# Last stage of a hybrid decoder step: who adds the expert outputs to the residual rows, VectorE or TensorE

## The reference, cut to what matters

```python
combine = (jax.nn.one_hot(g_idx, N_GROUPS)[:, :, None] * within[:, None, :] * g_w[:, :, None]).reshape(n, N_EXPERTS)
y = jnp.zeros((n, D_MODEL), jnp.float32)
for e in range(N_EXPERTS):
    hid = jax.nn.silu(t @ w_gate[e]) * (t @ w_up[e])
    y = y + combine[:, e:e + 1] * (hid @ w_down[e]).astype(jnp.float32)
...
xp = xp + hier_moe(rmsnorm(xp, norm_ffn_g[l]), *moe_args)
...
y_prompt = rmsnorm(xp, final_norm_g)
y_sample = rmsnorm(xs, final_norm_g)
```

## Time and profile before

| | |
|---|---|
| median of 3 runs | 716.06 us (715.21 to 717.71) |
| profiled execution | 715.4 us |
| its span, first to last instruction | 713.7 us |
| TensorE busy in the span | 692.3 us (97%) |
| VectorE, ScalarE, GpSimd busy | 555.3, 451.4, 152.3 us |
| mean granted TensorE clock | 0.997 |
| last matmul of the last expert, start of its group | 681.71 us |
| first load of `yy` issued | 687.89 us |
| last scaling ends, last store issued | 710.2 us |

### The profile page before, as it was taken

The page is one execution under the profiler, slowest core; times in us unless marked ns, Lnnn a source line. Parts: engine busy times, 40 slices in busy tenths (PEclk is TensorE's granted clock), DMA queues, the critical chain, the costliest instruction groups (busy, mean ns, idle before and its releaser), DMA issues.

```text
span 713.7 us, 11899 instructions
## 1 busy us (share of the span) xinstructions
PE 692.3 (97%) x3816; PEld 540.9 (76%) x3816; DVE 555.3 (78%) x890; ACT 451.4 (63%) x714; POOL 152.3 (21%) x157
## 2 busy tenths in 40 slices
PE   7999999999999999999988999999999999999995
PEld 4777777887778778777777888888888888888842
DVE  4775866866858875363887999999999999999857
ACT  7645354453465643122245888898889888898745
POOL 1010010110110131000014233333333333341114
PEclk9999999999999999999999999999999999999998
DMA  9993830330311626635339999999999999998758
GB/s 350 267 308 96 196 89 0 88 88 0 88 59 68 237 96 235 261 128 187 112 137 353 415 415 412 411 392 388 403 392 381 380 393 393 366 404 339 268 197 357
DMA packets 80922, 181.10 MB, mean 254 GB/s; under 512 B 41720, under 2 KB 45984, under 8 KB 72696
## 3 DMA queue, kind: packets, MB, share of 16 engines
q1 hardware_dynamic: 71384, 163.12, 63.0%
q0 software_dynamic: 9216, 16.93, 6.3%
q10 hardware_dynamic: 288, 0.62, 0.3%
HBM read 162.89 MB, written 34.39 MB: 276 GB/s over the span
## 4 chain that ended last, share of the span: by engine, by line
PE 85%; DVE 4%; DMA 4%; ACT 2%; issue 2%; SPq 1%; POOL 1%; DVEq 0%; ACTq 0%; POOLq 0%
PE psZ L1391 24%; PE psZ L901 20%; PE psS L1418 12%; PE psZ L1092 10%; PE psT L831 6%; PE psOG L831 2%; PE psOG L974 2%; PE psS L942 2%; DMA wo_in<-w_out 1%; PE psOG L1223 1%; PE psOG L983 1%; DMA yy<-y_d 1%; PE psOG L873 1%; DVE x1a L2692 1%; PE psT L1181 1%
## 5 line engine op out<-in xcount | busy, mean ns | idle before, releaser
L2388 DVE TENSOR_TENSOR wg_lo<-wg,wg_hi 128x1024 fp32r<-128x1024 f32 x128 | 150.7, 1218 | 2.0 <-ACT wg_hi L1531 2.0
L1531 ACT ACTIVATE wg_hi<-wg 128x1024 fp32r<-128x1024 f32 x128 | 128.8, 1062 | 3.6 <-DVE small L2550 1.6
L1391 PE MATMUL psZ<-wg_hi,xg_hi 128*128 128x512 f32 x252 | 101.4, 402 | 0.0
L1391 PE MATMUL psZ<-wg_hi,xg_lo 128*128 128x512 f32 x252 | 99.0, 393 | 0.0
L1391 PE MATMUL psZ<-wg_lo,xg_hi 128*128 128x512 f32 x252 | 99.0, 393 | 0.0
L901 PE MATMUL psZ<-wi_hi,xT_hi 128*128 128x512 f32 (+1 forms) x240 | 90.0, 375 | 1.0 <-DVE wi_lo L1963 1.0
L2774 POOL DMA_INDIRECT y_d<-y_t,idx_dst x32 | 48.9, 1528 | 188.5 <-ACT y_t L1531 188.5
L2577 DVE TENSOR_TENSOR wd_lo<-wd,wd_hi 128x2048 fp32r<-128x2048 f32 x31 | 71.1, 2292 | 21.0 <-ACT wd_hi L1531 21.0
L901 PE MATMUL psZ<-wi_lo,xT_hi 128*128 128x512 f32 (+1 forms) x240 | 87.2, 364 | 0.0
L901 PE MATMUL psZ<-wi_hi,xT_lo 128*128 128x512 f32 (+1 forms) x240 | 87.2, 363 | 0.0
L2770 POOL DMA_INDIRECT xg<-h_d,idx_src x32 | 58.5, 1830 | 22.2 <-issue 13.7
(11 more groups left out here) (354 smaller groups left out, 1346.3 us busy)
## 6 DMA issues: line engine op xcount, KB each, us to landing
wg<-w_gate SPq DMA_DIRECT2D x32, 1024.0 KB, 9.9
wg<-w_up SPq DMA_DIRECT2D x32, 1024.0 KB, 17.4
wd<-w_down SPq DMA_DIRECT2D x32, 1024.0 KB, 13.1
y_d<-wo_stage SPq DMA_DIRECT2D x1, 4608.0 KB
wi_raw<-w_in SPq DMA_DIRECT2D x4, 1024.0 KB, 14.1
x_t<-x_rows SPq DMA_DIRECT2D x8, 512.0 KB, 4.0
mix_d<-mix_t SPq DMA_DIRECT2D x8, 512.0 KB, 3.0
m_t<-mix_d SPq DMA_DIRECT2D x8, 512.0 KB, 3.7
```

What stands on the lines that cost most here:

```text
L1391: last = nc.tensor.matmul(psZ[z][:], a[:, c, :], w, start=(n == 0), stop=(n == 3 * DC - 1))
L1531: return nc.scalar.activation(out, in_, ACT.Copy)
L2388: tt(wg_lo[k][:, :, c, :], wg[k][:, :, c, :], wg_hi[p][:].bitcast(F32), ALU.subtract).then_inc(s_wgl, 1)
```

## The change

TensorE sums the tiles 4 to 8 in place of 5 to 8, but only x1 and the upper sum. All nine lower sums are made by VectorE, in place, before: those of tiles 4, 5 and 6 directly behind VectorE's last instruction for the experts (they wait for `s_ylo` alone), those of tiles 7, 0, 1, 2, 3 and 8 behind the wait `s_sct >= 1`. VectorE's value load of the expert count moves from ahead of the lower sums to behind the first three. Each lower sum raises `s_ysum` by one. TensorE copies x1 of the tiles 4 to 7 into the four pairs of banks, waiting for the lower sum of each, then adds the upper sums of the tiles 4 to 7, and then waits until VectorE has scaled tile 4 (`s_fo >= 5`), copies x1 of tile 8 into `psOG` again and adds its upper sum. ScalarE builds five diagonal matrices in place of eight. VectorE has no upper sum of tile 4 left, and scales tile 4 out of PSUM.

```diff
-SUM_PE = [5, 6, 7, 8]
+SUM_PE = [4, 5, 6, 7, 8]
+LOWER_FIRST = [4, 5, 6]
+LOWER_THEN = [7, 0, 1, 2, 3, 8]
...
-        sums = dict(zip(SUM_PE, (psOG, psT2, psS, psZ2)))
+        sums = dict(zip(SUM_PE, (psOG, psT2, psS, psZ2, psOG)))
...
+        def lower_done(i):
+
+            return (LOWER_FIRST + LOWER_THEN).index(i) + 1
...
+            def add_x1(j):
+                pe.wait_ge(s_ysum, lower_done(j))
+                add_rows(j, ident, x1(final_tile(j)[0]), True, False)
+
+            def add_upper(n, j):
+                pe.wait_ge(*upper(j))
+                add_rows(j, dg[:, n, :], yy[j], False, True).then_inc(s_fs, 1)
+
             pe.wait_ge(s_ya, NE)
-            pe.wait_ge(s_ylo, 16 * T)
-            for n, j in enumerate(SUM_PE):
-                add_rows(j, ident, x1(final_tile(j)[0]), True, False)
-                pe.wait_ge(s_dg, 1)
-                add_rows(j, dg[:, 0, n, :], y_lo[j], False, False)
-            for n, j in enumerate(SUM_PE):
-                pe.wait_ge(*upper(j))
-                add_rows(j, dg[:, 1, n, :], yy[j], False, True).then_inc(s_fs, 1)
+            for j in SUM_PE[:4]:
+                add_x1(j)
+            pe.wait_ge(s_dg, 1)
+            for n, j in enumerate(SUM_PE[:4]):
+                add_upper(n, j)
+
+            pe.wait_ge(s_fo, SUM_PE[0] + 1)
+            add_x1(T - 1)
+            add_upper(4, T - 1)
...
-            for k in range(2):
-                for n, j in enumerate(SUM_PE):
-                    t = final_tile(j)[0]
-                    last = nc.scalar.activation(dg[:, k, n, :], ident, ACT.Copy, scale=w_of[:, k, t:t + 1])
+            for n, j in enumerate(SUM_PE):
+                t = final_tile(j)[0]
+                last = nc.scalar.activation(dg[:, n, :], ident, ACT.Copy, scale=w_of[:, 1, t:t + 1])
...
-            most = dve.value_load(cnt_i[0:1, :], min_val=0, max_val=N_TOK)
             dve.wait_ge(s_ylo, 16 * T)
             dve.wait_ge(s_xs, 16 * 14)
+            for i in LOWER_FIRST:
+                add_lower(i, w_of[:, 0]).then_inc(s_ysum, 1)
+            most = dve.value_load(cnt_i[0:1, :], min_val=0, max_val=N_TOK)
             dve.wait_ge(s_sct, 1)
-            for i in range(T):
-                if i not in SUM_PE:
-                    last = add_lower(i, w_of[:, 0])
-            last.then_inc(s_ysum, 1)
+            for i in LOWER_THEN:
+                add_lower(i, w_of[:, 0]).then_inc(s_ysum, 1)
```

More of the change, by code:

```diff
@@ L318, in build @@
         fst = s6.take("fst", [P, T, 4], F32)
-        dg = s6.take("dg", [P, 2, len(SUM_PE), P], F32)
+        dg = s6.take("dg", [P, len(SUM_PE), P], F32)
         s6y = Region(nc, base, 0, 40960)
@@ L1492, in _ @@
                         down(wd[0], o_dn)
-                pe.wait_ge(s_ylo, 32 * T)
+                pe.wait_ge(o_step, (N_CHUNK - 1) * OV_LINKS + 2)
             def add_rows(j, lhsT, rhs, start, stop):
@@ L1928, in sq_final @@
                 else:
-                    act.wait_ge(s_ysum, i + 2 - sums_to(i))
+                    act.wait_ge(s_ysum, T + i + 1 - sums_to(i))
                     rows_ = x1(t)
@@ L2665, in _ @@
                 link.n = (N_CHUNK - 1) * OV_LINKS + 1
-                dve.wait_ge(s_ysum, 1)
+                dve.wait_ge(s_ysum, T)
                 dve.wait_ge(s_ylo, 32 * T)
                 for i in range(T):
-                    if i not in SUM_PE:
-                        last = add_lower(i, w_late)
+                    last = add_lower(i, w_late)
                 link(last)
             dve.wait_ge(s_sct, 2)
-            dve.wait_ge(s_ysum, 1)
+            dve.wait_ge(s_ysum, T)
             dve.wait_ge(s_gain, 48)
@@ L2688, in scale_rows @@
                 if i not in SUM_PE:
-                    dve.wait_ge(s_ysum, i + 2 - sums_to(i))
+                    dve.wait_ge(s_ysum, T + i + 1 - sums_to(i))
                 rows_ = sums[i] if i in SUM_PE else x1(t)
```

## The result

The change makes the kernel slower: 721.69 us (median of 5, 720.46 to 723.41) against 716.76, a ratio of 1.0072 with a 95% interval of 1.0055 to 1.0089. By the ratio that is 5.2 us where 2.8 were forecast, and 721.69 is outside the range given. The profiled execution took 720.46 us and its span is 717.8, 4.1 us more than before. The other four spans are 719.2 to 721.3 us, so the profiled one is the mildest of the five.

The account below looks back on a forecast made before the run. Bound before: last scatter, `yy` loads, then VectorE's last scalings, not TensorE. With the change TensorE ends last: 707.7 + 2.45 (clock) + 3.55 to the last scaling, + 2.15 + 0.6 storing = 716.5 span, 2.8 more; median 718.9, range 716.6 to 720.5.

Parts of the forecast that it names:

- Lower sums of tiles 4, 5, 6 at nothing: VectorE ahead of 684.52: three sums, 3.65 us, fit into 6.94 us of idle time; price 0.
- The other six at nothing but 1.2 us of VectorE, hidden: VectorE behind `s_sct`: six sums in place of five end at 691.8, hidden by sum 2's load wait, 0.3 us to spare.
- TensorE's pause lowers the clock: TensorE ahead of the upper sums: 6.1 us pause drops it to 1.2 GHz, loss 2.45 us (1.7 to 3.4); chance 0.72.
- Rival D: Loads of `yy` come earlier while TensorE pauses, making the kernel faster; a 3.5 us pause can't lower the clock; chance 0.05.
- Six groups in place of four: TensorE's upper sums: starting at 697.1, they end at 707.7 at full clock, 2.1 us later than before.
- Storing, 2.8 us from the last scaling to the end: End of kernel: without a backlog, 2.15 us for the last store plus 0.6, from 713.7 to 716.5.
- B: Rival: TensorE's clock stays up through the pause; 0.3 to 0.7 us more, or 716.4 to 716.8; chance 0.16.
- C: Rival: TensorE's clock falls and stays low to the end, losing 5.2 us in place of 2.45; 721.6; chance 0.07.

Follow-up runs that it names:

- e12: Kernel before with lower sums of tiles 1 to 4 run early on VectorE and the sample tile's behind the last scatter; ratio 1.0002.
- e6: Changed kernel with VectorE's six later lower sums started behind GpSimd's last scatter, not beside it; ratio 1.0040 against the kernel before.
- e15: Kernel before with VectorE's value load moved directly ahead of its wait for the last scatter's start; ratio 1.0101.
- e10: Kernel before with VectorE's five lower sums in the order 1, 2, 3, 4, 0, the 8-row sample tile last; ratio 1.0006.
- e1: Changed kernel with three more copies of x1 of tile 7 to keep TensorE busy in its pause; ratio 1.0051 against the kernel before.
- e14: Changed kernel with VectorE's value load moved back ahead of the first three lower sums; ratio 1.0069 against the kernel before.
- e7: Changed kernel with later lower sums behind the last scatter and three more copies of x1 of tile 7; ratio 1.0032 against the kernel before.
- e8: As e7, but TensorE sums only tiles 4 to 7 and VectorE adds tile 8's upper sum; ratio 1.0012 against the kernel before.
- e9: Kernel before with one more GpSimd memset behind its last power, for which nothing waits; ratio 1.0024.
- e3: Changed kernel with tile 8's power taken off GpSimd, using ScalarE's square root and VectorE's reciprocal; ratio 1.0112 against the kernel before.
- e2: Changed kernel with the sample tile's 8-row lower sum ahead of tile 7's behind the scatter's start; ratio 1.0197 against the kernel before.

## Why the prediction was wrong, point by point

*Lower sums of tiles 4, 5, 6 at nothing: right.* They ran from 679.27 to 682.95 below an idle engine, and the scatter beside them took 1.12 us. e12 shows the same on the kernel before: 1.0002.

*The other six at nothing but 1.2 us of VectorE, hidden: wrong, and the first step that failed.* I asked what the early sums do to the scatter of 681.58, but for the last scatter took over that the kernel before has a sum beside it at no cost. That row of before didn't carry over: there VectorE led by 0.07 us. In the changed kernel it leads by 0.17, the scatter takes 1.96, and the loads start 0.9 us later; tile 4 of `yy` lands at 697.7, not 697.1. In the profiled execution that is 0.75 us on TensorE's start. Starting the sums behind the scatter (e6) is worth 2.3 us by the medians, of which the traces explain 0.9, and one moved line that gives the kernel before the same 0.1 us more of lead costs it 7.2 us (e15). The Trainium skill (SBUF — State Buffer, Who interferes with whom) says that a VectorE instruction with two inputs in SBUF contends with a GpSimd instruction that reads SBUF, and that the order of issue decides who blocks, not the shape of the operation. The runs agree that the two contend. On who blocks they agree only in part: by the starts VectorE is first in all ten traces with a sum beside the scatter, in the kernel before and in e10 too, where the scatter isn't held, and what changes in e15 is the lead, from 0.07 to 0.18 us. At 0.07 us the shape changes nothing (e10); at 0.17 the runs with the 8-row sum first are held far longer than those with a 128-row sum first. And GpSimd stayed out for a whole row of instructions, 6.73 and 7.94 us of scatter, not only for the one that was running.

*TensorE's pause lowers the clock: right,* and so was its place on the path: fall 3.6 us after the last matmul (3.8 in the earlier trace rows), return 3.5 us after the new start. The loss was 3.69 - 1.98 = 1.7 us in the profiled execution, at the lower end of the 1.7 to 3.4 given for it, in place of 2.45. e1 takes it away. e6 and e14 lose 2.6 us in their profiled executions, so 2.45 was a fair price and the 1.7 one draw. By the medians the three pairs with and without the copies differ by 1.5, 0.6 and 0.1 us, which is inside the intervals. The moment of the fall, which no row of before could bound, varies: 2.2 us after the last matmul in e15 (its stretch of 703 to 704 has a mean of 0.64), 5.3 in e14. Rival D's remark that a pause of 3.5 us leaves the clock no time to fall need not hold.

*Six groups in place of four: right.* TensorE ended at 710.12 against a forecast of 710.15. That it is so close is luck: the two errors above, 0.75 us each, offset each other. The last scaling ended at 713.66 against 713.7. e7 to e8 puts the last two groups at some 0.2% of the time.

*Storing, 2.8 us from the last scaling to the end: wrong, the second step that failed.* The store itself was right: SyncE was done at 715.9, 2.2 us after the last scaling. But the end is the drain of GpSimd, 5.3 us behind its last power. It gave 4.1 us, 1.3 more than forecast. It was there before, 0.3 us behind the landing of the last store, and no row that I read showed it, as the page doesn't count such instructions as busy and the chain of waits names the last scaling. Two signs could have been read: SyncE's queue waited 0.3 us for something else behind its last store, and the forecast moved GpSimd's last instruction by 4 us while shortening the storing by 0.65. e9 and e3 show the drain from both sides.

*The size.* Against the profiled span the sum is 2.8 + 1.3 (drain) + 0.75 (scatter) - 0.75 (clock) = 4.1, what was measured. The other 1.1 us up to the median's 5.2 lies in executions that were not traced, and its cause stays open. For the scatter speaks that e6 gains 2.3 us by the medians, against it that the scatter took the same 1.96 or 1.97 us in all five traces with this order. For the clock speaks that three of the four other executions have a mean granted clock of 0.989 where the profiled one has 0.993, that e6 and e14 lose 0.9 us more to it, and that e10's trace has it at 0.5 also inside the expert loop, from 373.7 to 380.5; against it, that the slowest execution (723.41) has 0.994.

*The rivals.* Nothing spoke for B or C: the clock fell and came back. D was reversed: the loads came later, not earlier.

## What to carry to other kernels

When a helper engine's DMA issue overlaps work of VectorE at no cost, ask how close the two starts are: here 0.1 us of VectorE's start goes with 0.97 us or 7, and starting the work behind the issue (e6) took the delay away. Look at the end of the program as at an engine of its own: what each engine still does behind its last instruction can be hidden by the last store and come out as soon as that engine's last work moves. And an engine that sums on the side at 2.4 GHz is paid for by what keeps it busy ahead: work taken away from it in a wait for loads may come back at half speed when the loads are there (3.69 us for a group of 1.98).

## What the runs showed of the hardware that I had not expected

- GpSimd's closing drain lasts until 5.3 us after the end of its last instruction, with a last instruction of 0.10 us as with one of 0.55.
- GpSimd's indirect DMA was held for 0.99, 5.8 and 7.0 us beside VectorE's sums of three operands, one after the other without a gap, and let in only at a boundary or at the end of the row. It got in at the first boundary in the five traces that begin with a 128-row sum and at none in e2 and e15, which begin with the 8-row one; why stays open.
- VectorE's first instruction behind a semaphore started 0.05 us after GpSimd's instruction that raises it where the early sums or the value load stood just ahead (after, e14, e15), and 0.16 us after where neither did (before, e10). The cause stays open.
- After the last matmul ahead of a wait for loads, the clock fell from 2.4 to 1.2 GHz 3.6 us later in the changed kernel, 2.2 us later in e15 and 5.3 us later in e14.
- ScalarE's square root and its square didn't share a table: each change cost a load of 1.28 us.
